# Value matmuls placed ahead of the request groups in a two-layer hybrid decoder step

## The reference

```
xn  = rmsnorm(x, norm1_g);  z = xn @ w_in            # 1024 -> 2448 columns
o_a = forgetting attention  (4 heads of 64, causal, softmax(q k / 8 + F_q - F_k))
o_b = conformer: glu -> depthwise conv of 31 taps -> layernorm -> silu
o_c = native sparse attention: compressed + 16 selected blocks + window of 512, gated
o_d = u * (per-chunk mixing of layernorm(v))
h   = x + concat_g(rmsnorm(o_g)) @ w_out
y   = h + relu(rmsnorm(h, norm2_g) @ w_ff1)**2 @ w_ff2
```

## Time and profile before

| | us |
|---|---|
| median of 3 runs | 3452.82 (3451.35 to 3454.71) |
| the profiled execution | 3454.09 |
| its span in the trace | 3452.3 |
| PE (TensorE) busy | 3270.9 |
| DVE (VectorE) busy | 1449.1 |
| ACT (ScalarE) busy | 1013.4 |
| mean granted clock of TensorE | 0.984 of full |

### The profile page before, as it was taken

One profiled execution on the slowest core, in us unless ns is written; L12 is line 12 of the kernel. 1 busy time (PEld: TensorE's weight loads), 2 busy tenths in 40 slices (PEclk: granted clock), 3 DMA queues, 4 the chain that ended last, 5 costly groups with the idle time before them and its releaser, 6 DMA issues.

```text
span 3452.3 us, 55746 instructions
## 1 busy us (share of the span) xinstructions
PE 3270.9 (95%) x22444; PEld 1884.6 (55%) x22642; DVE 1449.1 (42%) x2779; ACT 1013.4 (29%) x1804; POOL 229.4 (7%) x172
## 2 busy tenths in 40 slices
PE   8999989888899999999999998989888999999998
PEld 4555466666654444444445555666666444444444
DVE  5965643333544311332169566433336532113312
ACT  2123344444433300231102233444444322013211
POOL 1211200000200000000002111000011000000000
PEclk9999999999899999999999999999999999999999
DMA  8423334333221211113153324334323112111322
GB/s 270 115 91 105 108 103 145 116 97 114 77 74 49 64 46 31 49 55 93 50 150 105 105 79 144 125 99 136 127 63 110 44 48 73 43 31 43 79 74 90
DMA packets 375956, 312.53 MB, mean 91 GB/s; under 512 B 121565, under 2 KB 358649, under 8 KB 368377
## 3 DMA queue, kind: packets, MB, share of 16 engines
q1 hardware_dynamic: 367912, 208.59, 21.5%
q0 software_dynamic: 7840, 101.20, 7.9%
HBM read 264.34 MB, written 50.46 MB: 91 GB/s over the span
## 4 chain that ended last, share of the span: by engine, by line
PE 88%; DVE 5%; ACT 4%; issue 2%; SPq 1%; POOL 0%; DMA 0%; POOLq 0%; DVEq 0%; ACTq 0%
PE PS L922 45%; PE PS L1041 14%; PE PS L1309 5%; PE PS L1332 5%; PE PS L1200 3%; PE PS L954 2%; PE PS L1358 2%; PE PS L1016 2%; ACT arena L1617 1%; PE PS L1246 1%; PE PS L1388 1%; PE PS L1207 1%; DVE arena L2189 1%; PE PS L1002 1%; PE PS L1212 1%
## 5 line engine op out<-in xcount | busy, mean ns | idle before, releaser
L922 PE MATMUL PS<-arena 128*128 128x512 bf16 (+1 forms) x9882 | 1538.4, 316 | 10.4
L922 PEld LDWEIGHTS PS<-arena 128*128 128x128 bf16 x10080 | 753.4, 98 | 794.8
L1041 PE MATMUL PS<-arena 128*128 128x512 f32 (+3 forms) x1152 | 480.5, 573 | 3.2 <-DVE arena L1922 3.2
L1493 ACT ACTIVATE arena<-arena 128x1024 bf16<-128x1024 f32 (+1 forms) x108 | 141.4, 1310 | 1089.3 <-PE PS L922 1076.0
L1041 PEld LDWEIGHTS PS<-arena 128*128 128x128 f32 (+1 forms) x1152 | 209.4, 185 | 241.7 <-issue 208.7
L2503 DVE TENSOR_TENSOR arena<-PS,arena 128x1088 f32<-128x1088 f32 (+1 forms) x48 | 62.0, 1292 | 643.1 <-PE PS L922 632.0
L1309 PE MATMUL PS<-arena 128*128 128x512 f32 (+3 forms) x576 | 237.2, 520 | 8.6 <-ACT arena L1626 3.9
L2529 DVE SCALAR_TENSOR_TENSOR arena<-PS,arena 128x1088 f32<-128x1088 f32 x64 | 82.7, 1292 | 353.2 <-PE PS L922 352.7
L1332 PE MATMUL PS<-arena 128*128 128x64 f32 x1632 | 216.0, 278 | 0.0
L1332 PEld LDWEIGHTS PS<-arena 128*128 128x128 f32 x1632 | 204.6, 198 | 4.9 <-DVE arena L2405 1.7
L2189 DVE COPY arena<-PS 128x128 f32<-128x128 f32 (+3 forms) x136 | 68.4, 503 | 300.4 <-PE PS L1358 300.2
(11 more groups left out here) (355 smaller groups left out, 2886.4 us busy)
## 6 DMA issues: line engine op xcount, KB each, us to landing
arena<-in_w_ff SPq DMA_DIRECT2D x64, 512.0 KB, 4.2
arena<-in_w_ff SPq DMA_DIRECT2D x32, 1024.0 KB, 5.7
arena<-in_cache_nsa_kv SPq DMA_DIRECT2D x256, 64.0 KB
x_s<-arena SPq DMA_DIRECT2D x24, 544.0 KB, 3.5
arena<-in_w_in SPq DMA_DIRECT2D x4, 2048.0 KB, 14.8
arena<-in_w_out SPq DMA_DIRECT2D x16, 512.0 KB, 4.7
arena<-x_s SPq DMA_DIRECT2D x2, 3264.0 KB, 10.3
arena<-in_w_in SPq DMA_DIRECT2D x12, 512.0 KB, 6.7
```

Source lines behind the costliest of these rows:

```text
L922: last = mm(PS[:, 1536 * k + a:1536 * k + a + wd], ww[:, c, :], xx[:, c, a:a + wd], start=c == 0 and n == 0, stop=c == blocks - 1 and n == 2)
L1041: last = mm(PS[0:r, c * 512:c * 512 + b - a], XNT[:, j, t * P:t * P + r], Wt[:, j, a:b], start=j == 0, stop=j == KD - 1)
L1493: run(WH[k][:, 0:blocks, :], src[k][:, 0:blocks, :], ACT.Copy).then_inc(S["w_hi"], 1)
```

## The change

Six edits. In the stream the values of unit u-1 stand right behind the transposes of unit u, ahead of the unit's other groups. `mx` and `ex` of a request are split: the forgetting branch (part 0) has its maxima behind `ds` 3 in unit 4 of the request and its exponent at the head of unit 5, the other two branches stay in unit 7. `lateness` and `later_sums` move from unit 5 to unit 7. Of the merge groups `mw` goes behind `oa` of tile 2, and the norm `gn` 4 one unit later. In the gate stage VectorE runs 10 instead of 16 half taps ahead of the last value evacuation and 12 instead of 6 behind it. `state_T` goes from ahead of the products (f=0, s=1) to ahead of (f=1, s=0), on TensorE alone.

```diff
-                    4: [ds(3)], 5: [kt(8), kt(9)], 6: [ds(4), kt(10), ds(5), kt(11)],
-                    7: [ds(6), kt(12), ds(7), ds(8), ("mx", b), ("ex", b)], 8: [("pt", b, 0), ("pt", b, 1), ("pt", b, 2)],
+                    4: [ds(3), ("mx", b, 0)], 5: [("ex", b, 0), kt(8), kt(9)], 6: [ds(4), kt(10), ds(5), kt(11)],
+                    7: [ds(6), kt(12), ds(7), ds(8), ("mx", b, 1), ("ex", b, 1)], 8: [("pt", b, 0), ("pt", b, 1), ("pt", b, 2)],
...
-                     LAST + 4: [("mw",), ("oa", 2, 0), ("oa", 2, 1)], LAST + 5: [("mo", 0), ("mo", 1), ("gn", 3), ("gn", 4)],
-                     LAST + 6: [("mo", 2), ("oa", 3, 0), ("oa", 3, 1)], LAST + 7: [("oa", 4, 0), ("oa", 4, 1)]}.get(u, [])
+                     LAST + 4: [("oa", 2, 0), ("oa", 2, 1), ("mw",)], LAST + 5: [("mo", 0), ("mo", 1), ("gn", 3)],
+                     LAST + 6: [("mo", 2), ("oa", 3, 0), ("oa", 3, 1), ("gn", 4)], LAST + 7: [("oa", 4, 0), ("oa", 4, 1)]}.get(u, [])
...
-        TAPS_GLU, TAPS_FIRST, TAPS_TILE = 22, 9, (4, 3, 4)
+        TAPS_AHEAD, TAPS_GLU, TAPS_FIRST, TAPS_TILE = 10, 22, 9, (4, 3, 4)
...
                         if f == 0 and s == 1:
                             pe.wait_ge(S["col_mean"], 1)
+                        if f == 1 and s == 0:
                             state_T()
...
-                    elif u == 5:
+                    elif u == 7:
                         lateness()
...
+                    if u >= 1:
+                        values(u - 1)
                     for key in extras_of(u):
                         if key[0] not in BANKLESS:
                             extra(key)
-                    if u >= 1:
-                        values(u - 1)
...
-                        b = key[1]
-                        act.wait_ge(S["dmx"], b + 1)
-                        for n, x in enumerate((SF, SSL, SW)):
+                        b, part = key[1:]
+                        act.wait_ge(S["dmx"], 2 * b + part + 1)
+                        for n, x in ((1, SSL), (2, SW)) if part else ((0, SF),):
                             run(x, x, ACT.Exp, bias=MALL[:, n, b:b + 1], accum_out=LALL[:, n, b:b + 1]).then_inc(S["dex"], 1)
...
-                        for half in HALF_TAPS[:TAPS_GLU - 6]:
+                        for half in HALF_TAPS[:TAPS_AHEAD]:
...
-                        for half in HALF_TAPS[TAPS_GLU - 6:TAPS_GLU]:
+                        for half in HALF_TAPS[TAPS_AHEAD:TAPS_GLU]:
...
-                        dve.wait_ge(*evacuated(GROUP_AT["ds", b, 8]))
-                        V.reduce_max(MALL[:, :, b], MX, AX, negate=True).then_inc(S["dmx"], 1)
+                        part = key[2]
+                        dve.wait_ge(*evacuated(GROUP_AT["ds", b, 8 if part else 3]))
+                        g = slice(1, 3) if part else slice(0, 1)
+                        V.reduce_max(MALL[:, g, b], MX[:, g, :], AX, negate=True).then_inc(S["dmx"], 1)
...
-                    elif u == 5:
+                    elif u == 7:
                         later_sums()
```

More of the change, by code:

```diff
@@ L2337, in request_out @@
                             if b:
-                                dve.wait_ge(S["dmx"], b)
+                                dve.wait_ge(S["dmx"], 2 * b)
                         if s == 4 and b == 0:
```

## The result

The changed kernel takes 3401.1 us (median of 4 runs, 3390.5 to 3407.7), the kernel before 3452.1 beside it: a ratio of 0.9848, 95% interval 0.9820 to 0.9877, so 51 us or 1.5% faster (42 to 62). The prediction was 3384 us (3358 to 3432). The profiled execution took 3397.0 us, 57.1 less than the profiled one of before; predicted for that pair were 69.

What follows compares the result with a forecast made beforehand. TensorE, busy 3270.9 of 3452.3 us, was taken as the bound, waiting in the attention streams for single answers. Terms 42 + 8 + 4 + 4 + 1 + 10 = 69 us off 3454.1, less 1.3 for the median: 3384 us, range 3358 to 3432.

Steps and rivals of the forecast that it cites:

- values ahead: Attention streams: value matmuls cover copy latency; of 60 us pauses, 8 set aside, 10 kept back, 42 gained; bounds 0 and 60.
- exponent: Attention streams: forgetting branch's exponent leaves ScalarE's burst before the probabilities' transposes; 8 us gained, bounds 0 and 14.7.
- lateness + merge: Page-lateness product and merge groups: moved steps shorten TensorE's waits, 4 of 7.2 us and 4 of 9.
- gate stage: First layer's gate stage: two waits go, a new one comes at the mixing matrices; 1 us gained, bounds +4 and -3.
- clock: Both attention streams: fewer half-clock stretches after stalls the change touches; 10 us gained, bounds 0 and 27.
- The reserve of 10: Attention streams: 10 us of the 60 us of pauses kept back for new waits at the unit's end.
- rival (b): Unit's end in the streams: wait moves to the next unit's second bank, 0.5 us a unit; 3476 us, chance 0.04.
- Rival (a): Attention streams: pauses are ScalarE's and VectorE's arrears, so moving values shortens nothing; 3431 us, chance 0.09.
- My sign of being wrong: Attention streams: forecast is wrong if the exponents' burst still holds TensorE for over 1.5 us.
- about half goes: Merge groups: a later norm and multiplication remove 4 of 9 us of waits at L1271 and L1140.
- the clock falls as often as before: TensorE's clock in the new profile: if this is seen, the forecast is wrong.
- Rival (d): TensorE's clock: stalls under 3 us do not cause its falls, which come anyway; sum 59, 3394 us, chance 0.12.

Runs made afterwards that it cites:

- the three pauses in the dense stage: Changed kernel with GpSimd operations making TensorE pause three times in each layer's last stage (1.73, 3.28 and 7.46 us); 3433.5 us, one run.
- the last kernel: The change without its gate stage edits, plus a separate count for page loads and later head's sums; 3380.1 us, ratio 0.9791 to the kernel before.

## Why the prediction was right, and where it was not

| step | predicted us | alone, timed (95%) | alone, at full clock |
|---|---|---|---|
| values ahead | 42 | 31 (24 to 37) | 40 |
| exponent | 8 | 10 (6 to 15) | 7 |
| lateness + merge | 4 + 4 | 3 (-2 to 8) | 1 |
| gate stage | 1 | 1 (-5 to 6) | -2 |
| clock | 10 | | none |
| all | 69 | 51 (42 to 62) | 54 |

**Values.** The mechanism held: the short waits for a copy went where the values cover it. The size, 42 for 40, is in part luck, for three errors cancel. I had 60 us of pauses, of them some 15 in the smaller rows; those rows hold 23.9, so the pauses were 68. I set 8 aside as ScalarE's arrears, and these were right as a kind, since the waits that stayed in the kernel with the values alone are the long ones, but too few: all copy rows lost 34.5 us, not 52. What made up for it is the time that a pause costs beyond its own row (14 us by the estimate above), which I did not have. The reserve of 10 was for waits at the unit's end, which did not come: no wait of L1359 for L1618 or L2190 appears among the changed kernel's rows, and rival (b) fell with that. It was used up elsewhere, by the page loads (7.2 us with the values alone), which the prediction did not look at: it had asked what the engines would be late for, not what SyncE's queue would. I had expected 415 us for the stream window and under 20 us for the copy waits of those rows; 424.7 and 22.4 came, both short of it.

**Exponent.** Half of 16 us was taken, and 7 to 10 came, in L1233 and the longest waits of L1091 as said. Rival (a), that the pauses are all arrears and moving values shortens nothing, fell with the values alone (31 us) and with the kernel that had everything but them (11 us). My sign of being wrong, the burst still holding TensorE for over 1.5 us, was just met: 1.51 at 745.7.

**Lateness and merge.** The step that failed is "about half goes". For lateness I named the wait that follows, and in the changed kernel it was 2.5 us a layer against the estimated 2, of 3.6; net 2 instead of 4. With these two parts alone it was 0.4 us a layer at most, so there, by the rows, the 4 was too low. In the merge 5.5 us of waits went and 7.2 came: I named the later multiplication as what might be waited for instead, and it was the group norm, which `oa`'s transposes now reach too early, that was. The lower bound (-2) held, the value of 4 did not. Together the two measure 3 (-2 to 8), 1 at full clock, for 8.

**Gate stage.** Every event was right: TensorE at the mixing matrices early (102.7 us, estimated 105), a wait to 111.2 (estimated 111.3), a slow restart. The restart was sized about right too: 2 us in the changed kernel, 2 to 3 in the six kernels with the edits, for the 2 that I set aside. The term that was mis-sized is the 3.0 us won ahead of the mixing matrices: 2.2 in the profiled pair (91.5 to 89.3), and nothing against the other kernels without the edits, whose clock came back sooner there than in the profile I read. So the edit costs 2.4 us instead of giving 1, inside the bounds (+4 to -3). And behind VectorE's chain, which I took for the bound, stands a second one some 3 us shorter, SyncE's issue of 64 small loads.

**Clock.** This is the step that was wrong. "Seven such falls in the first layer's stream follow stalls that the change touches" was true, and they did go; but six others came, in or behind the stalls of 2.7 us that were left and behind ones of 1.2 to 1.6. In the two streams together 61 us are at half clock now, where 51 were. My own test, "the clock falls as often as before", is met. The mean clock of the changed kernel was 0.983 and that of the kernel before 0.984 to 0.985 in the timed runs: if anything some 3 us lost, instead of 10 won. Without the clock the sum is 59, and the profiled pair, both at a mean of 0.984, shows 57. Rival (d) gave the better number, 3394, though for a reason that the pauses only half bear out: two stalls of 1.73 us in dense work were harmless, and in the stream the clock fell behind 1.20. The Trainium skill (TensorE: Matmul & The Clock Gate, section Why this matters for your kernels), which warns of idle gaps over about 3 us, agrees with the three pauses in the dense stage and not with the fall behind 1.20 us in the stream.

**Sums.** The bounds of the terms add up to 122 us better (60 + 14.7 + 7.2 + 9 + 4 + 27), not to the 132 of the prediction; the stated range did not use it. At full clock the parts measured alone give 40 + 7 + 1 - 2 = 46 us, and all together 54: the 8 between them belong to no single part.

## What to carry to other kernels

Where an engine waits for the copy of its own result, put work that depends on neither between producing and reading it; the same work one place earlier bought nothing here. Long waits in such rows are another engine's burst and need that burst split: sort a row by its longest wait before pricing it. After the first big wait goes, look at the queue that only issues transfers, since it was never late before; and do not book the clock's recovery as a gain for stalls that go while others stay: here 48 us of copy waits went, and the time at half clock stayed at 114 of 115 us.

## What was not expected of the hardware

- Two kernels with nearly the same work differed by 0.0075 in mean clock (0.9802 for values and exponent, 0.9877 for the last kernel), 20 to 25 us of 3400, with the kernel before at 0.984 beside both. Differences of under 10 us between such kernels could be read only from spans times clock.
- In the long stalls here the clock fell while TensorE was still idle, and only the rest of the half-clock stretch cost time. Of the 10.2 us around the 8.55 us stall at the mixing matrices 4.1 lay in work, and of the 10.2 around each 7.46 us pause in the dense stage 5.2 and 5.0; behind a pause of 3.28 us it was 3.0 or nothing.
- The issue of a load took SyncE 0.39 us for the small ones of fixed address (58 in 22.34 us, L667) and 0.38 for the window right behind the pages (L751), but 1.27 for a page, whose address is read from a table first (16 in 20.38 us, L748). Which part of the 1.27 is the reading was not tried.
